# Two tables of step order changed: modulation products apart from their transposing products, selections and gates at other places

## The chip, the cores and the metric

The kernel runs on one core of a Trainium2 chip, as one program with one launch. The metric is the device time of that program in microseconds; lower is better. The engines are TensorE (PE, matrix products), VectorE (DVE), ScalarE (ACT), GpSimd (POOL) and SyncE (SP, which only issues transfers here). Each runs its own queue in order; they wait for one another on semaphores.

## The reference, cut to what matters

Two blocks on 256 latent tokens (and 256 context tokens) of width 1024, all in fp32.

The first block has two layers. In each, `silu(c) @ w_ada + b_ada` gives shift, scale and gate (the modulation); tokens are modulated and projected with `w_in`; then come three mixers: attention (8 heads on 2 key heads, RMS norm, rotary angles, softmax), a gated linear attention (GLA) forward and backward with log decays, and a gated spatial unit (SGU). Their outputs are multiplied by branch matrices and by sigmoid gates, summed, multiplied by `w_out`, and normed with the residual:

```
h = x * (1.0 + scale) + shift
y_attn, y_gla, y_sgu = attention(h), gla_forward(h) + gla_backward(h), sgu(h)
m = sigmoid(ga) * (ya @ w_br_attn) + sigmoid(gg) * (yg @ w_br_gla) + sigmoid(gs) * (ys @ w_br_sgu)
x = layer_norm(ALPHA * x + gate * (m @ w_out))
```

Layer 0 does this for latent and context tokens (512 in all); layer 1 only yields the latent ones, though keys, values and decays are still needed for all 512. The second block is a mixer (forgetting attention and a linear recurrence) and a mixture of 32 experts.

## The kernel before, in words

Four parts run one after the other: trunk layer 0, trunk layer 1, the mixer, the experts. Only the two trunk layers are touched.

A trunk layer is a list of named steps, built by `trunk_schedule(l)`: a fixed head, then the words of the table `ORDER_0` or `ORDER_1`, then the merging and closing steps. Each engine walks through the same list and issues what its own part of each step asks for; so the table sets the order on every engine at once. A step that an engine has no part in costs it nothing. The engines are not in step with each other: a step's parts are joined by semaphores alone.

Weights come from a stream of halves of 1 MB, fetched by SP into a ring of four. Its order is made from the tables too (`stream_order`: first use). Each dense weight is split into two parts: ACT copies the high part (L221), DVE subtracts it to get the residue (L229; four of them go to POOL). `with_splits` places these `split` steps two uses ahead of the product, and never before an `ada` step that stands ahead of that product. A dense product is then three products (L247, L248, L249).

PSUM has three pools of banks, taken in turn in the order in which TensorE opens them: four `proj` banks (PJ), two `score` banks (PS), two `turn` banks (PT). TensorE waits at an opening until the bank's last user has been copied out. So a step's place in the table also says which earlier job it has to wait for.

The steps that the change and the prediction speak of:

- `ada.l.n` (L702): a product with the modulation weights, in a PT bank; ACT copies its row out (L929). `adat.l.n` (L712): small products that turn this row into columns, in the next PT bank, after ACT's copy; DVE adds the bias (L1109). Layer 0 also does those of layer 1.
- `ag, ak, gq, gate, aq, gk, av, gv, sv, sg, su, gg`: dense products with parts of `w_in`; ACT copies most of them out, DVE `su`.
- `z`, `soft`, `decay`: the log decays; `soft` is a logarithm on ACT over 2048 elements (L1026), `decay` a subtraction and eight scans on DVE (L1173, L1179).
- `stat`, `rstd`, `rot`: head norms (a product, then logarithm L1000/L1004 and exponential L1009 on ACT, a product on DVE L1187) and the rotary products (L753, L1192 to L1195).
- `score.i` (L763): two products of queries and keys, in PS banks; DVE takes the minimum of the negated scores (L1200), ACT the exponential (L1034). `sums.i`: a reciprocal. `turn.i` (L771): transposes in PT banks, copied by ACT (L1043). `pv.i` (L783, L787): the product with the values. Layer 0 has 16 of these units (the last eight are twice as wide), layer 1 has 8.
- `key`, `keymul`, `keyt`, `kv`: the keys and the states of the GLA.
- `diag.p`, and for 14 numbers i (seven levels of two halves) `diff.i` (DVE L1261 and L1262, POOL L1366 and L1367, then two exponentials on ACT, L1060), `scale.i` (DVE L1265, POOL L1373), `pairs.i` (PE L826, DVE blends it in, L1276). `diff.i` has to wait for `pairs.(i-2)`, since it overwrites its operands.
- `svstat`, `svn`, `mix`: the norm and the product of the SGU. `query`, `out`, `ostat`, `orstd`, `silu`, `ysplit`, `merge_gate`: the end of the GLA and the beginning of the merging.

ACT holds one table of functions at a time; a change of function may put a load (ACT_TABLE_LOAD) in front of an instruction.

Of the kernel before, what the change touches and what calls it, by code (L numbers as in the profile page):

```python
# [410 lines left out]


ORDER_0 = """
ag.0 ag.1 ag.2 ag.3 ak.0 gq.0 gq.1 gate.0 aq.0 z.0 aq.1 z.1 stat.0 aq.2 z.2 aq.3 z.3 gk.0 stat.1 stat.2 gk.1
stat.3 stat.4 soft.0 av.0 rstd.0 rstd.1 rstd.2 rstd.3 rstd.4 gv.0 rot.0 rot.2 rot.3 decay.0 rot.1 gv.1 rot.4
decay.1 vt.0 gv.2 score.0 key.0 keymul.0 gv.3 sums.0 score.1 turn.0 sv.0 keyt.0 key.1 sv.1 keymul.1 ada.0.4
adat.0.4 sums.1 turn.1 sv.2 keyt.1 kv.0 kv.1 sv.3 svstat.0 kv.2 score.2 svn.0 pv.0 score.3 sg.0 sums.2 diag.0
turn.2 pv.1 sg.1 score.4 diag.1 sums.3 turn.3 sg.2 sg.3 pv.2 diff.0 score.5 sums.4 turn.4 scale.0 diff.1 pv.3
score.6 sgsilu.0 sums.5 diff.2 scale.1 pairs.0 turn.5 pv.4 su.0 score.7 scale.2 pairs.1 diff.3 sums.6 turn.6
ada.0.5 adat.0.5 pairs.2 pv.5 scale.3 diff.4 score.8 sums.7 mix.0 turn.7 scale.4 pairs.3 diff.5 score.9 su.1  # L420
sums.8 scale.5 pv.6 pairs.4 diff.6 ada.1.0 turn.8 adat.1.0 pv.7 score.10 scale.6 pairs.5 diff.7 sums.9 turn.9
pv.8 mix.1 su.2 scale.7 pairs.6 diff.8 score.11 sums.10 turn.10 scale.8 pairs.7 diff.9 pv.9 ada.1.1 adat.1.1
score.12 sums.11 pairs.8 scale.9 diff.10 turn.11 mix.2 pv.10 score.13 scale.10 pairs.9 diff.11 sums.12 su.3
turn.12 pv.11 scale.11 turn.13 pairs.10 diff.12 score.14 ada.1.2 adat.1.2 sums.13 scale.12 pairs.11 pv.12
mix.3 score.15 sums.14 diff.13 scale.13 ada.1.3 adat.1.3 pairs.12 turn.14 pv.13 sums.15 pairs.13 turn.15
ada.1.4 adat.1.4 pv.14 pv.15 query.0 ada.1.5 adat.1.5 ysplit.s.0 ysplit.s.1 ysplit.s.2 ysplit.s.3 gg.0 gg.1
out.0 silu.0 silu.1 out.1 ostat.0 ostat.1 gg.2 ostat.2 ostat.3 gg.3 orstd.0 orstd.1 orstd.2 orstd.3 silu.2
silu.3 merge_gate.s.0
"""


ORDER_1 = """
ak.0 gq.0 gq.1 gate.0 aq.0 z.0 aq.1 z.1 aq.2 z.2 aq.3 stat.1 stat.2 z.3 stat.0 gk.0 gk.1 stat.3 stat.4 soft.0
av.0 rstd.0 rstd.1 rstd.2 rstd.3 rstd.4 rot.1 rot.4 rot.0 rot.2 rot.3 vt.0 decay.0 decay.1 score.0 key.0
score.1 keymul.0 gv.0 gv.1 gv.2 gv.3 sums.0 keyt.0 key.1 turn.0 score.2 keymul.1 sv.0 sv.1 sv.2 sv.3 svstat.0
svn.0 keyt.1 kv.0 sums.1 sums.2 turn.1 kv.1 kv.2 diag.0 diag.1 pv.0 diff.0 scale.0 score.3 diff.1 mix.0
scale.1 turn.2 pairs.0 diff.2 pv.1 scale.2 pairs.1 score.4 diff.3 mix.1 diff.4 sums.3 scale.3 pairs.2 turn.3
scale.4 pv.2 pairs.3 diff.5 score.5 mix.2 sums.4 scale.5 pairs.4 turn.4 diff.6 scale.6 pv.3 pairs.5 diff.7
score.6 mix.3 scale.7 sums.5 pairs.6 diff.8 turn.5 scale.8 pairs.7 pv.4 diff.9 scale.9 score.7 pairs.8 sums.6
diff.10 scale.10 turn.6 pairs.9 diff.11 pv.5 scale.11 pairs.10 sums.7 diff.12 scale.12 turn.7 pairs.11 diff.13  # L440
pv.6 scale.13 pairs.12 pv.7 pairs.13 query.0 ysplit.s.0 ysplit.s.1 gg.0 gg.1 silu.0 silu.1 ysplit.s.2
ysplit.s.3 out.0 out.1 ostat.0 ostat.1 gg.2 ostat.2 ostat.3 gg.3 orstd.0 orstd.2 orstd.1 orstd.3 silu.3
merge_gate.s.0 silu.2
"""


# [1947 lines left out]
```

How the kernel before makes its waits and increments, by code:

```python
    def open(self, pe, name):  # L123
        n, size = len(self.job), len(self.tiles)
        assert name not in self.job, name
        self.job[name] = n
        if n >= size:
            pe.wait_ge(self.evac_sem[n % size], n // size)
        return self.tiles[n % size]
# [46 lines left out]
    def issue(self, sp, upto):  # L176
        upto = min(upto, len(STREAM))
        for n in range(self.issued, upto):
            if n >= NHALF:
                sp.wait_ge(*self.last_reader[n - NHALF])
            sp.dma_start(self.ring[:, n % NHALF, :], self.dram[n]).then_inc(self.landed[n % NHALF], 16)
        self.issued = max(self.issued, upto)
# [31 lines left out]
    def hi(self, act, slot, c):  # L215
        n = self.index[slot, c]
        kind = self.info[n][2]
        act.wait_ge(*self.W.has_landed(slot, c // 2))
        if n >= NPIECE:
            act.wait_ge(*self.used[n - NPIECE])
        act.activation(self.part(self.hi_ring[:, n % NPIECE, :], kind), self.raw(slot, c, kind), ACT.Copy)\
            .then_inc(self.hi_written, 1)
# [1 line left out]
    def lo(self, eng, name, slot, c):  # L224
        n = self.index[slot, c]
        _, _, kind, engine, _ = self.info[n]
        if engine == name:
            eng.wait_ge(self.hi_written, n + 1)
            eng.tensor_tensor(self.part(self.lo_ring[:, n % NPIECE, :], kind), self.raw(slot, c, kind),
                              self.part(self.hi_ring[:, n % NPIECE, :], kind).bitcast(F32), ALU.subtract)\
                .then_inc(self.lo_written[engine], 1)
```

## Time and profile before

| | us |
|---|---|
| median of 3 runs | 1442.76 |
| the three runs | 1442.76, 1439.63, 1442.8 |
| profiled execution | 1438.7 |
| its span, first to last instruction | 1436.9 |
| mean granted TensorE clock in it | 0.965 |
| PE / DVE / ACT / POOL busy | 1336.2 / 630.7 / 517.8 / 68.3 |
| layer 0, layer 1 (start to end, about) | 0 to 641, 641 to 1014 |
| mixer and experts (about) | 1014 to 1437 |

The times in the views are microseconds from the start of the span. A row of a timeline gives start, duration, engine, line, what is written and read, how many instructions are merged, and in brackets the idle time before it and what ended that. The granted clock is 1.00 at 2.4 GHz and 0.50 at 1.2 GHz, the only two levels in this trace; a mean between them mixes both.

### The profile page before, as it was taken

The numbers are of one execution on the slowest core, as the hardware profiler recorded it, in microseconds if no ns is written. First come the engines' busy times: TensorE is split into PE (matmuls) and PEld (weight loads), VectorE is DVE, ScalarE is ACT, GpSimd is POOL, SyncE is SP. The second block draws the span as 40 slices with busy tenths as digits, with TensorE's granted clock in tenths as the row PEclk, the third lists the DMA queues.
The fourth block names the chain that finished last, engine by engine and source line by source line (L and its number), as shares of the span: only waits on it lengthen the run. The fifth ranks groups of instructions, "written<-read, shape, count | busy, mean of one in ns | idle before, by whom it ended". The sixth has DMA issues, their size and how long they took to land. (4 is left out here: it accounts for less than half of the span.)

```text
span 1436.9 us, 19322 instructions
## 1 busy us (share of the span) xinstructions
PE 1336.2 (93%) x7954; PEld 1013.0 (70%) x7954; DVE 630.7 (44%) x1093; ACT 517.8 (36%) x877; POOL 68.3 (5%) x92
## 2 busy tenths in 40 slices
...
PEclk6999999898999999999998999999999999999998
...
GB/s 387 205 59 88 117 88 1 147 90 223 99 88 88 88 177 110 95 95 141 129 114 30 89 1 123 197 208 176 87 98 97 323 185 372 411 405 400 422 366 31
DMA packets 34222, 238.97 MB, mean 166 GB/s; under 512 B 4304, under 2 KB 4432, under 8 KB 6224
## 3 DMA queue, kind: packets, MB, share of 16 engines
...
q14 instruction: 28, 0.23, 0.0%
HBM read 236.59 MB, written 1.05 MB: 165 GB/s over the span
## 5 line engine op out<-in xcount | busy, mean ns | idle before, releaser
L229 DVE TENSOR_TENSOR pieces_lo<-weight_ring,pieces_hi 128x1024 fp32r<-128x1024 f32 x154 | 188.0, 1224 | 322.0 <-ACT pieces_hi L221 321.9
L247 PE MATMUL proj<-h_hi,pieces_hi 128*128 128x512 f32 (+1 forms) x816 | 289.4, 355 | 7.6 <-DVE h_lo L1145 3.6
L248 PE MATMUL proj<-h_lo,pieces_hi 128*128 128x512 f32 (+1 forms) x816 | 282.9, 347 | 0.0
L249 PE MATMUL proj<-h_hi,pieces_lo 128*128 128x512 f32 (+1 forms) x816 | 281.6, 345 | 0.0
L221 ACT ACTIVATE pieces_hi<-weight_ring 128x1024 fp32r<-128x1024 f32 x158 | 165.9, 1053 | 112.5 <-PE score L249 50.6
L247 PEld LDWEIGHTS proj<-h_hi,pieces_hi 128*128 128x128 f32 x816 | 154.7, 190 | 37.7 <-issue 10.5
L248 PEld LDWEIGHTS proj<-h_lo,pieces_hi 128*128 128x128 f32 x816 | 155.0, 190 | 21.2 <-issue 1.7
L249 PEld LDWEIGHTS proj<-h_hi,pieces_lo 128*128 128x128 f32 x816 | 155.2, 190 | 20.7
L1943 PE MATMUL turn<-expert_parts,e_gathered 128*64 128x256 f32 x768 | 85.3, 379 | 0.8 <-DVE e_gathered L2132 0.8
L1943 PEld LDWEIGHTS turn<-expert_parts,e_gathered 128*64 128x64 f32 x768 | 56.0, 137 | 32.4 <-issue 7.3
L1078 ACT ACTIVATE l_merge_gate<-proj 128x512 f32<-128x512 f32 (+1 forms) x48 | 23.6, 491 | 130.4 <-PE proj L249 130.4
L247 PE MATMUL proj<-pieces_hi,h_hi 128*128 128x512 f32 x160 | 65.7, 411 | 1.1 <-ACT l_probs_t L985 0.9
L248 PE MATMUL score<-l_y_lo,pieces_hi 128*128 128x512 f32 (+1 forms) x192 | 64.7, 337 | 0.0
L247 PE MATMUL score<-l_y_hi,pieces_hi 128*128 128x512 f32 (+1 forms) x192 | 64.4, 335 | 0.0
L249 PE MATMUL proj<-pieces_hi,h_lo 128*128 128x512 f32 x160 | 64.3, 402 | 0.0
L248 PE MATMUL proj<-pieces_lo,h_hi 128*128 128x512 f32 x160 | 64.2, 401 | 0.0
L249 PE MATMUL score<-l_y_hi,pieces_lo 128*128 128x512 f32 (+1 forms) x192 | 64.1, 334 | 0.0
L1503 PE MATMUL proj<-x_hT,weight_ring 128*128 128x256 f32 x256 | 58.2, 387 | 0.0
L1503 PEld LDWEIGHTS proj<-x_hT,weight_ring 128*128 128x128 f32 x256 | 49.4, 195 | 7.7 <-issue 0.8
L2143 DVE SCALAR_TENSOR_TENSOR e_out_lo<-score,e_slot_combine,e_out_hi 128x512 fp32r<-128x512 f32 x32 | 24.0, 751 | 52.8 <-ACT e_out_hi L2022 52.8
L2136 DVE TENSOR_TENSOR e_hidden<-e_silu,turn 128x256 f32<-128x256 f32 x16 | 6.7, 422 | 91.2 <-ACT e_silu L2010 91.2
L1034 ACT ACTIVATE l_probs<-score,l_small 128x512 f32<-128x512 f32 (+1 forms) x48 | 29.0, 609 | 43.9 <-DVE l_small L1200 43.8
(439 smaller groups left out, 2042.8 us busy)
## 6 DMA issues: line engine op xcount, KB each, us to landing
weight_ring<-in_stream SPq DMA_DIRECT2D x110, 1024.0 KB, 4.8
...
weight_ring<-in_experts SPq DMA_DIRECT2D x26, 1024.0 KB, 11.2
...
l_q<-in_ada_first SPq DMA_DIRECT2D x1, 1024.0 KB, 10.1
```

Source lines behind the costliest of these rows:

```text
L221: act.activation(self.part(self.hi_ring[:, n % NPIECE, :], kind), self.raw(slot, c, kind), ACT.Copy)\
L229: eng.tensor_tensor(self.part(self.lo_ring[:, n % NPIECE, :], kind), self.raw(slot, c, kind), self.part(self.hi_ring[:, n % NPIECE, :], ki ...
L247: pe.matmul(out, sh, mh, start=start, stop=False)
L248: pe.matmul(out, sh, ml, start=False, stop=False)
L249: return pe.matmul(out, sl, mh, start=False, stop=stop)
L1034: act.activation(PR[:, i % 2, u, 0:n], PS.tile(J("score", i, u))[:, 0:n], ACT.Exp, bias=small[:, i % 2, u:u + 1], scale=-1.0, accum_out=sm ...
L1078: act.activation(SGM[:, n % 4, 0:NT], PJ.tile(J("merge_gate", i))[:, 0:NT], ACT.Sigmoid)\
L1503: last = pe.matmul(acc[:, 0:T], w[:, k, i * P:(i + 1) * P], hT[:, k, :], start=(k == 0), stop=(k == KT - 1))
L1943: last = pe.matmul(acc[64 * f:64 * f + 64, u * 256:(u + 1) * 256], XG[:, q % 2, k, slots], w[:, n, f * 256:(f + 1) * 256], start=(k == 0), ...
L2136: dve.tensor_tensor(HG[:, i % 2], HS[:, i % 2], up, ALU.mult).then_inc(*PT.evac(J("gu", i)))
L2143: dve.scalar_tensor_tensor(OUT_L[:, i % 2, c], PS.tile(J("out", i, h))[:, :], CS[:, i // 4 % 2, i % 4:i % 4 + 1], OUT_H[:, i % 2, c].bitca ...
```

## The change

Only the two tables change. Both hold the same words as before. In layer 0 the moves are, in the main:

- `ak.0` and `gq.0` go ahead of `ag.2` and `ag.3` (this swaps two halves of the weight stream); `gk.1`, `aq.3`, `av.0` and the `z` and `stat` steps between them are arranged anew; `soft.0` goes between `rstd.3` and `rstd.4`.
- `turn.1` goes between `ada.0.4` and `adat.0.4`; `pairs.12` and `turn.14` between `ada.1.3` and `adat.1.3`; `pv.15` between `ada.1.5` and `adat.1.5`.
- `pairs.1` and `diff.3` go ahead of `su.0` and `score.7`; `score.8` ahead of `pv.5`; `turn.9` ahead of `score.10`; `score.11` behind `pv.9`; `mix.3` ahead of `pairs.11`; many `sums`, `scale` and `diff` steps by a few places.
- `query.0` goes behind `gg.0`, three of four `ysplit.s` behind `silu.0`, `orstd.0` behind `orstd.2`.

In layer 1: `decay.1` behind `score.0`; `keyt.0` ahead of `gv.3`; `keymul.1` behind `sv.0`; `diag.1` behind `pv.0`; `mix.1` and `diff.4` behind `pairs.2`; `diff.6` ahead of `turn.4` and `scale.5`; `diff.10` ahead of `sums.6`; `silu.3` behind `merge_gate.s.0`.

The lines of the diff that hold these moves (the rest of both tables is left out):

```diff
 ORDER_0 = """
-ag.0 ag.1 ag.2 ag.3 ak.0 gq.0 gq.1 gate.0 aq.0 z.0 aq.1 z.1 stat.0 aq.2 z.2 aq.3 z.3 gk.0 stat.1 stat.2 gk.1
-stat.3 stat.4 soft.0 av.0 rstd.0 rstd.1 rstd.2 rstd.3 rstd.4 gv.0 rot.0 rot.2 rot.3 decay.0 rot.1 gv.1 rot.4
-decay.1 vt.0 gv.2 score.0 key.0 keymul.0 gv.3 sums.0 score.1 turn.0 sv.0 keyt.0 key.1 sv.1 keymul.1 ada.0.4
-adat.0.4 sums.1 turn.1 sv.2 keyt.1 kv.0 kv.1 sv.3 svstat.0 kv.2 score.2 svn.0 pv.0 score.3 sg.0 sums.2 diag.0
-turn.2 pv.1 sg.1 score.4 diag.1 sums.3 turn.3 sg.2 sg.3 pv.2 diff.0 score.5 sums.4 turn.4 scale.0 diff.1 pv.3
-score.6 sgsilu.0 sums.5 diff.2 scale.1 pairs.0 turn.5 pv.4 su.0 score.7 scale.2 pairs.1 diff.3 sums.6 turn.6
-ada.0.5 adat.0.5 pairs.2 pv.5 scale.3 diff.4 score.8 sums.7 mix.0 turn.7 scale.4 pairs.3 diff.5 score.9 su.1
...
+ag.0 ag.1 ak.0 gq.0 ag.2 ag.3 gq.1 gate.0 aq.0 z.0 aq.1 stat.0 z.1 aq.2 z.2 z.3 gk.0 stat.1 aq.3 stat.3 av.0
+stat.4 stat.2 rstd.0 rstd.1 rstd.2 rstd.3 gk.1 soft.0 rstd.4 gv.0 rot.2 rot.3 decay.0 rot.1 rot.4 gv.1 rot.0
+decay.1 vt.0 gv.2 score.0 key.0 keymul.0 gv.3 sums.0 score.1 turn.0 sv.0 keyt.0 key.1 sums.1 sv.1 keymul.1
+ada.0.4 turn.1 adat.0.4 sv.2 keyt.1 kv.0 kv.1 sv.3 svstat.0 kv.2 score.2 svn.0 pv.0 score.3 sg.0 sums.2 sg.1
+pv.1 diag.0 turn.2 diag.1 sums.3 turn.3 sg.2 score.4 sg.3 pv.2 diff.0 score.5 sums.4 turn.4 scale.0 diff.1
+pv.3 score.6 sums.5 sgsilu.0 pairs.0 diff.2 scale.1 turn.5 pv.4 scale.2 pairs.1 diff.3 su.0 score.7 sums.6
+turn.6 ada.0.5 adat.0.5 pairs.2 scale.3 score.8 sums.7 pv.5 mix.0 turn.7 pairs.3 sums.8 diff.4 diff.5 scale.4
+score.9 su.1 scale.5 pairs.4 pv.6 diff.6 ada.1.0 turn.8 adat.1.0 pv.7 turn.9 scale.6 score.10 pairs.5 diff.7
+pv.8 mix.1 sums.9 su.2 scale.7 pairs.6 diff.8 turn.10 scale.8 sums.10 pairs.7 diff.9 pv.9 score.11 sums.11
+scale.9 ada.1.1 adat.1.1 score.12 pairs.8 diff.10 turn.11 sums.12 mix.2 pv.10 score.13 scale.10 pairs.9
...
+pv.12 sums.13 score.15 sums.14 diff.13 ada.1.3 pairs.12 scale.13 turn.14 adat.1.3 pv.13 pairs.13 turn.15
+ada.1.4 sums.15 adat.1.4 pv.14 ada.1.5 pv.15 adat.1.5 gg.0 query.0 ysplit.s.0 gg.1 out.0 silu.0 ysplit.s.1
+ysplit.s.2 ysplit.s.3 silu.1 out.1 ostat.0 ostat.1 gg.2 ostat.2 ostat.3 gg.3 orstd.1 orstd.2 orstd.0 orstd.3
+silu.2 silu.3 merge_gate.s.0
 """
 ORDER_1 = """
...
-av.0 rstd.0 rstd.1 rstd.2 rstd.3 rstd.4 rot.1 rot.4 rot.0 rot.2 rot.3 vt.0 decay.0 decay.1 score.0 key.0
-score.1 keymul.0 gv.0 gv.1 gv.2 gv.3 sums.0 keyt.0 key.1 turn.0 score.2 keymul.1 sv.0 sv.1 sv.2 sv.3 svstat.0
-svn.0 keyt.1 kv.0 sums.1 sums.2 turn.1 kv.1 kv.2 diag.0 diag.1 pv.0 diff.0 scale.0 score.3 diff.1 mix.0
-scale.1 turn.2 pairs.0 diff.2 pv.1 scale.2 pairs.1 score.4 diff.3 mix.1 diff.4 sums.3 scale.3 pairs.2 turn.3
-scale.4 pv.2 pairs.3 diff.5 score.5 mix.2 sums.4 scale.5 pairs.4 turn.4 diff.6 scale.6 pv.3 pairs.5 diff.7
...
+av.0 rstd.0 rstd.1 rstd.2 rstd.3 rstd.4 rot.1 rot.4 rot.0 rot.2 rot.3 vt.0 decay.0 score.0 decay.1 key.0
+score.1 keymul.0 gv.0 gv.1 gv.2 keyt.0 gv.3 sums.0 key.1 turn.0 score.2 sv.0 keymul.1 sv.1 sv.2 sv.3 svstat.0
+svn.0 keyt.1 kv.0 sums.1 sums.2 turn.1 kv.1 kv.2 diag.0 pv.0 diag.1 diff.0 scale.0 score.3 diff.1 mix.0 turn.2
+scale.1 pairs.0 diff.2 pv.1 scale.2 pairs.1 score.4 diff.3 sums.3 scale.3 pairs.2 mix.1 diff.4 turn.3 scale.4
+pv.2 pairs.3 diff.5 score.5 mix.2 pairs.4 diff.6 turn.4 sums.4 scale.5 scale.6 pv.3 pairs.5 diff.7 score.6
...
+out.0 out.1 ostat.0 ostat.1 gg.2 ostat.2 ostat.3 gg.3 orstd.0 orstd.2 orstd.1 orstd.3 merge_gate.s.0 silu.3
+silu.2
 """
```

## Rows read from the trace of the kernel before

**Rows 1.** The page: busy time by engine, and PE's clock in 40 slices.
```profile
PE 1336.2 (93%) x7954; PEld 1013.0 (70%) x7954; DVE 630.7 (44%) x1093; ACT 517.8 (36%) x877; POOL 68.3 (5%) x92
...
PEclk6999999898999999999998999999999999999998
```

**Rows 2.** Stretches: length, then busy PE, PEld, DVE, ACT, POOL; PEclk, DMA share, GB/s.
```profile
34.60:129.60 95.00, 95.00 (x379) 71.29 (x379) 26.56 (x31) 42.68 (x54) 0.00 (x0) 0.98 0.34 128
...
200.20:231.10 30.90, 30.90 (x186) 24.06 (x184) 13.41 (x28) 9.05 (x21) 0.00 (x0) 0.98 0.10 35
...
243.90:259.80 15.90, 11.86 (x61) 6.74 (x61) 7.21 (x16) 4.17 (x9) 3.44 (x5) 0.57 0.31 120
...
389.80:641.00 251.20, 251.10 (x1096) 203.42 (x1096) 108.19 (x125) 71.29 (x89) 0.00 (x0) 1.00 0.29 103
757.00:772.00 15.00, 6.78 (x14) 3.11 (x15) 13.45 (x28) 4.95 (x12) 0.00 (x0) 0.54 0.00 0
...
820.00:860.00 40.00, 32.24 (x343) 24.19 (x341) 36.42 (x110) 25.13 (x65) 20.20 (x40) 1.00 0.01 2
```

**Rows 3.** Waits of PE over the span: total us, times, longest.
```profile
PE turn L712 <- ACT l_y_gla L929: 11.6, 11, 2.4
PE score L763 <- ACT l_probs L1034: 8.3, 2, 7.3
```

**Rows 4.** Timeline of layer 1, 761 to 770 us, PE and DVE.
```profile
767.19 2.74 PE L763 MATMUL score<-l_k,l_q 64*128 64x512 f32 x4 [7.29 <-ACT l_probs L1034]
...
761.71 1.22 DVE L1173 TENSOR_TENSOR l_b_bwd<-l_b_bwd,l_decayed 128x1024 f32<-128x1024 f32 x1
762.97 2.63 DVE L1179 TENSOR_TENSOR_SCAN l_b_bwd<-consts,l_b_bwd 128x128 f32<-128x128 f32 x8
765.64 1.29 DVE L1200 TENSOR_REDUCE l_small<-score 128x1 f32<-128x512 f32 x2
```

**Rows 5.** Timeline of layer 1, PE: turn.0 and pv.0.
```profile
794.60 0.63 PE L771 MATMUL turn<-consts,l_probs 128*128 128x128 f32 x4 [0.50 <-ACT l_gla_att L1055]
...
818.48 1.09 PE L783 MATMUL proj<-l_probs_t,l_v 128*64 128x128 f32 x16 [0.92 <-issue]
```

**Rows 6.** Timeline of layer 0, PE: second half of turn.1.
```profile
177.13 0.41 PE L771 MATMUL turn<-consts,l_probs 128*128 128x128 f32 x2 [2.18 <-DVE modulation L1109]
```

**Rows 7.** Timeline of layer 0, ACT's load before rstd.0, PE's rot.1.
```profile
130.32 1.28 ACT L1009 ACT_TABLE_LOAD   x1
...
138.57 0.67 PE L753 MATMUL turn<-l_q,consts 128*128 128x256 f32 x2 [0.46 <-DVE l_probs L1192]
```

**Rows 8.** Timeline of layer 0, 233 to 255 us, PE, POOL and DVE.
```profile
233.44 1.16 PE L826 MATMUL proj<-l_decayed 64*128 64x128 f32 x16
...
235.61 0.39 PE L787 MATMUL proj<-consts,l_inverse_sums 128*64 128x128 f32 x4
...
236.03 1.47 POOL L1373 TENSOR_TENSOR l_decayed<-l_decayed,l_gla_k 128x512 f32<-128x512 f32 x1
...
236.27 1.78 DVE L1265 TENSOR_TENSOR l_decayed<-l_decayed,l_gla_q 128x512 f32<-128x512 f32 x1
...
247.23 3.64 PE L702 MATMUL turn<-weight_ring,silu_c 128*32 128x512 f32 x16 [3.32 <-ACT l_probs_t L1043]
...
253.38 2.08 PE L826 MATMUL proj<-l_decayed 64*128 64x128 f32 x16
```

**Rows 9.** Timeline of layer 0, PE: ada.1.1 and adat.1.1.
```profile
296.45 1.92 PE L702 MATMUL turn<-weight_ring,silu_c 128*32 128x512 f32 x16 [0.97 <-ACT l_probs_t L1043]
299.71 1.05 PE L712 MATMUL turn<-consts,l_y_gla 128*128 128x2 f32 x8 [1.33 <-ACT l_y_gla L929]
```

**Rows 10.** Timeline of layer 0, PE: adat.1.3 and pairs.12.
```profile
337.31 1.05 PE L712 MATMUL turn<-consts,l_y_gla 128*128 128x2 f32 x8 [2.21 <-ACT l_y_gla L929]
338.30 2.08 PE L826 MATMUL proj<-l_decayed 64*128 64x128 f32 x16
```

**Rows 11.** Timeline of layer 0, PE: start of gg.0.
```profile
356.54 0.47 PE L247 MATMUL proj<-h_hi,pieces_hi 128*128 128x512 f32 x1 [1.24 <-DVE pieces_lo L229]
```

More of the change, by code:

```diff
@@ L419 @@
-score.6 sgsilu.0 sums.5 diff.2 scale.1 pairs.0 turn.5 pv.4 su.0 score.7 scale.2 pairs.1 diff.3 sums.6 turn.6
-ada.0.5 adat.0.5 pairs.2 pv.5 scale.3 diff.4 score.8 sums.7 mix.0 turn.7 scale.4 pairs.3 diff.5 score.9 su.1
-sums.8 scale.5 pv.6 pairs.4 diff.6 ada.1.0 turn.8 adat.1.0 pv.7 score.10 scale.6 pairs.5 diff.7 sums.9 turn.9
-pv.8 mix.1 su.2 scale.7 pairs.6 diff.8 score.11 sums.10 turn.10 scale.8 pairs.7 diff.9 pv.9 ada.1.1 adat.1.1
-score.12 sums.11 pairs.8 scale.9 diff.10 turn.11 mix.2 pv.10 score.13 scale.10 pairs.9 diff.11 sums.12 su.3
```

14 lines of the change are left out of this document (4 added, 10 removed).

## The prediction, made before the change was run

> **What bounds the kernel now.** I read the page first. TensorE is busy for 93% of the span and its clock stands at full speed nearly throughout; DVE and ACT are busy for 44% and 36% [rows 1]. So only two things can be won: TensorE's waits, and the stretches at half clock. Next came the table by stretches [rows 2]. From 34.6 to 129.6 us, from 200.2 to 231.1 and in the whole closing part of layer 0 (389.8 to 641) TensorE is busy without a gap: 95.00 of 95.00, 30.90 of 30.90, 251.10 of 251.20. Reordering there can't pay. Between 243.9 and 259.8 it is busy for 11.86 of 15.90 us, at a mean clock of 0.57; between 757 and 772 for 6.78 of 15 us, at 0.54; between 820 and 860 for 32.24 of 40 us, while DVE is busy for 36.42 of 40: there DVE sets the pace. The list of waits puts 11.6 us on transposing products that wait for the copied modulation row, and 8.3 on score products that wait for ACT's exponential [rows 3]. The timelines then give the single places. No transfer ends one of these waits; the two swapped halves of the weight stream are both fetched at the start, so I put the swap at nothing.
>
> **Layer 1, the selection apart from the decay.** Score.1 sits 7.29 us waiting for a bank. ACT can free it only after DVE's minimum of score.0, and that one starts at 765.64, behind both decays. decay.1 begins at 761.71 and is 1.22 + 2.63 us. The table now puts score.0 ahead of it: 765.64 - 761.71 = 3.9 us earlier [rows 4]. What is then behind decay.1 on DVE (key.0, the minimum of score.1, keymul.0) is wanted by TensorE only behind gv.0 and gv.1, dense steps of 24 instructions at 0.23 us each by the closing part (251.10 for 1096) [rows 2], some 5.6 us. Against the 3.9: gv.0 starts at 765.9 instead of 769.9, in a clock that was half until 771.7 in this trace, so it may run at half for up to 4 us longer (a loss of 2.0) or get its clock back sooner (no loss). I take 0.6, so 3.3 net; bounds 1.9 and 3.9.
>
> Smaller places of layer 1. keyt.0 ahead of gv.3 lets its copies lie under gv.3: the 0.50 in front of turn.0 goes. pv.0 ahead of diag.1 removes 0.92 on TensorE, but DVE, which sets the pace from there, gains only its 0.4 [rows 5]. In the level loop diff.6 before scale.5, and diff.10 before sums.6, fill short DVE waits; DVE is idle for only 3.6 us of these 40 [rows 2], so 0.6, between 0 and 1. silu.3 behind merge_gate.s.0 saves a table switch where nobody waits: 0. Layer 1 together: 3.3 + 0.5 + 0.4 + 0.6 = **4.8**.
>
> **Layer 0, six places.**
> (a) ada.0.4, turn.1, adat.0.4. Now: 0.72 for the row copy (the smallest and commonest of the eleven waits of [rows 3]), then 2.18 because turn.1's second bank waits until DVE, behind two weight residues, has added the bias [rows 6]. Apart: turn.1.0 lies under the copy, but adat.0.4 now waits for ACT's copy of turn.1.0, which stands behind two weight splits. By the rows adat ends near 176.8 where turn.1 ended at 177.5: 0.7 gained, not 2.9. Bounds 0 and 2.3; the upper one adds that the clock, half after this wait, stays up.
> (b) soft.0 is put between rstd.3 and rstd.4. It is a logarithm among exponentials, and ACT loads a table of 1.28 us when it goes from one to the other. Two more loads delay rstd.4, and the residue of gv.2 and rot.2 behind it on DVE, by about 1.0 us (soft.0 and gk.1's copy no longer lie ahead of it in free time). TensorE has just gv.0 to hide this; the rot products wait 0.46 already. I take a loss of 1.0, between 0 and 2.6 (both loads) [rows 7].
> The Trainium skill, "ScalarE: Activation LUTs", section "Table sets: the hidden batching unit", says that one set holds both exp and ln, so that going from one to the other needs no further load. By that (b) would be free and the sum 1.0 better. The row shows the load between them here, so the measurement decides.
> (c) pairs.1 moves ahead of su.0. TensorE is free at 236.0, but pairs.1 needs POOL's product (ends 237.50) and DVE's (1.78 us beside POOL's, begun at 236.27). With pairs.0's blend put first on DVE it is ready between 237.65 and 238.45. I take 238.4: a new wait of 2.4 us. In return diff.3 and its exponential lie under su.0, ACT reaches turn.6 sooner, and the wait of 3.32 before ada.0.5 shrinks to 1.2. These two cancel (ada.0.5 at 247.8 instead of 247.2, a loss of 0.5). The gain, if any, is clock: after the 3.32 it was half until 259.7, where pairs took 2.08 instead of 1.16 and ada 3.64 instead of about 1.92; over the seven steps that is 5.5 us [rows 8, 2]. But the new wait of 2.4 may cost su.0 1.6, and 1.2 + 0.72 of waits with a thin transposing product between are still there. I take +3.0; bounds -2.1 and +5.5.
> The Trainium skill, "SBUF — State Buffer", section "Who interferes with whom", says that a DVE instruction with two SBUF inputs is shut out while GpSimd reads SBUF. By that DVE's difference and product would both come after 237.50, pairs.1 would be ready at 238.6 and the sum 0.2 worse; the 1.78 of the row fits it, but no row has this new order.
> (d) score.11 goes behind pv.9. ada.1.1 loses its 0.97 of wait, but ACT now copies its row behind diff.9 and score.11, and score.11 stands later. adat.1.1 follows near 10.1 us after su.2, against 9.5 now: -0.5, between -2 (a longer fall of the clock) and 0 [rows 9].
> (e) ada.1.3 and its transposing product: pairs.12 and the first half of turn.14 fit into the 2.21 of wait; both are ready. Some 0.5 of wait is left, so 1.7 is gained; and pairs.12 took 2.08, not 1.16, in the half clock that followed, turn.14 1.73 instead of 1.09: with the clock up 3.1. I take 3.0, bounds 1.7 and 3.1 [rows 10].
> (f) pv.15 between ada.1.5 and its product fills the 0.72, and ada.1.5 stands 1.3 earlier, so the residue of gg.0, on which 1.24 us are spent, comes earlier too: 1.2, bounds 0.7 and 1.4 [rows 11]. query.0 and three ysplits, now later on ACT, have gg.0 and gg.1 (11 us) for cover. If that cover went, out.0 would wait for two exponentials and two products, about 4 us.
> Everything else in layer 0 (ag and ak swapped, z and stat, gk.1, score.4, turn.9, the sums) lies where TensorE has no wait, or under a dense product: 0.
> Layer 0: 0.7 - 1.0 + 3.0 - 0.5 + 3.0 + 1.2 = **6.4**.
>
> **Sum.** 4.8 + 6.4 = 11.2 us. The profiled execution took 1438.7 (span 1436.9 and 1.8 around it) and would take 1427.5. It lies 4.1 below the median of the runs, 1442.76, which would become 1431.6. I name the middle, **1429.5**; on this scale the kernel before stands at 1440.7. The likeliest case's own range is 1424 to 1435. The mixer and the experts are unchanged and only start earlier.
>
> **Rivals.**
> 1. The clock stays up. A wait of 0.97 was passed at full speed in this trace, ada.1.1 taking 1.92 behind it [rows 9]; those of 2.2 and more were followed by half clock, as pairs.12 and pairs.2 show by 2.08 [rows 10, 8]. If (c) keeps it (+2.5), (a) too (+1.5), and (b) costs nothing (+1.0) with layer 1 at its upper bound (+0.6): 5.6 better, 1424. Against it: the new 2.4 in (c).
> 2. The waits only change places. Apart or not, adat waits for the same ACT queue; (a), (c) and (d) show that a step put between meets the next bank. If all of layer 0 comes to nothing and layer 1 gives only its lower bound of 1.9: 1438.8, no change.
> 3. Slower, by one mechanism: the clock. If it falls at the new wait before pairs.1 and stays half past 250, as it did after the 3.32, then (c)'s gain of 3.0 is lost, and 0.5 + 5.5 comes on top; the same persistence after (d)'s 2.6 us costs 4 more instead of 0.5 (3.5 net), and after score.0 the remaining 1.4. 11.2 - 3.0 - 6.0 - 3.5 - 1.4 = -2.7: about 1443.5. It decides at the first pairs behind su.0: 2.08 or 1.16. For it: the fall that lasted 16 us. Against it: the shorter falls of this trace ended within one or two steps, and a dense su.0 follows here.
>
> **Chances.** Forecast 0.45, rival 1 0.22, rival 2 0.20, rival 3 0.13. Differences below 0.3% (4.3 us) can't be told from no change. Forecast and rival 1 are faster, with a third of rival 2: 0.73; the rest of rival 2 and a part of rival 3: 0.18; slower 0.09. The range 1418 to 1442 takes in both ends of (c) and of layer 1.
>
> **What would show it.** In the profile after: the wait before score.1 of layer 1 at 3.4 us, not 7.3; a new wait near 2 before pairs.1 of layer 0, and ada.0.5's at 1.2; pairs.2 at 1.16; before adat.1.3 under 0.6; before adat.1.1 about 2.6; turn.1's second half released by ACT; a wait of about 1 between the rots. Wrong would be: pairs.2 again at 2.08, gv.0 of layer 1 beginning later than 8 us after score.0, or gv.1 of layer 0 more than 2 us late.

## The result, and the profile after

The changed kernel ran at 1425.62 us median of four runs (1425.14 to 1430.01), beside 1442.13 for the kernel before (four runs, 1439.63 to 1442.8): ratio 0.9911, 95% interval 0.989 to 0.9932, so 13 us faster by that ratio (the two medians alone lie 16.5 apart). The profiled execution took 1425.68 with a span of 1423.9, which is 13.0 less than the profiled one of before. A second set of six runs gave 1426.94 beside 1438.54 (0.9917, 0.9887 to 0.9947). The forecast was 1429.5.

The page of the kernel after: busy time by engine, and PE's clock in 40 slices (to set beside [rows 1]).

```profile
PE 1332.7 (94%) x7954; PEld 1013.1 (71%) x7954; DVE 629.9 (44%) x1093; ACT 519.1 (36%) x878; POOL 66.4 (5%) x92
...
PEclk7999999999999999998998999999999999999998
```

The same 7954 products; their busy time fell by 3.5 us, the rest of the 13.0 is waiting that went. The stretches of after: length, then busy PE, PEld, DVE, ACT, POOL; PEclk, DMA share, GB/s.

```profile
743.00:760.60 17.60, 13.12 (x28) 6.71 (x29) 17.10 (x41) 2.39 (x6) 0.00 (x0) 0.52 0.00 0
...
820.00:850.00 30.00, 23.91 (x257) 19.07 (x256) 27.25 (x81) 18.65 (x48) 14.12 (x28) 1.00 0.01 2
389.80:632.90 243.10, 243.10 (x1065) 197.21 (x1064) 104.59 (x122) 66.81 (x84) 0.00 (x0) 1.00 0.29 104
228.10:259.10 31.00, 25.55 (x205) 17.83 (x204) 20.90 (x44) 17.76 (x38) 11.24 (x14) 0.94 0.14 52
```

The closing part of layer 0 is still full. The stretch from the last gate to score.9 in layer 0 (228.1 to 259.1) now has a clock of 0.94. The same steps of before took 34.46 us, from 228.3 to 262.8; the stretch at a clock of 0.57 [rows 2] lies within them. The neighbourhood of layer 1's first scores is still at half clock (0.52).

The waits of PE, summed over the span (total, times, longest):

```profile
PE turn L712 <- ACT l_y_gla L929: 9.8, 8, 3.2
...
PE score L763 <- ACT l_probs L1034: 4.3, 2, 3.3
```

The waits of the transposing products fell by 1.8 us from 11.6, those of the scores by 4.0 from 8.3 [rows 3]: score.1's wait went from 7.29 to 3.26. Its timeline, PE and DVE:

```profile
755.37 2.74 PE L763 MATMUL score<-l_k,l_q 64*128 64x512 f32 x4 [3.26 <-ACT l_probs L1034]
...
753.81 1.29 DVE L1200 TENSOR_REDUCE l_small<-score 128x1 f32<-128x512 f32 x2
755.01 1.22 DVE L1173 TENSOR_TENSOR l_b_bwd<-l_b_bwd,l_decayed 128x1024 f32<-128x1024 f32 x1
```

DVE's minimum of score.0 now stands ahead of the second decay [rows 4]. In layer 0, around the new place of pairs.1:

```profile
235.26 0.39 PE L787 MATMUL proj<-consts,l_inverse_sums 128*64 128x128 f32 x4
238.03 1.84 PE L826 MATMUL proj<-l_decayed 64*128 64x128 f32 x16 [2.38 <-DVE l_decayed L1265]
239.80 0.79 PE L247 MATMUL proj<-h_hi,pieces_hi 128*128 128x512 f32 x1
...
249.02 1.92 PE L702 MATMUL turn<-weight_ring,silu_c 128*32 128x512 f32 x16 [1.25 <-ACT l_probs_t L1043]
251.66 1.05 PE L712 MATMUL turn<-consts,l_y_gla 128*128 128x2 f32 x8 [0.72 <-ACT l_y_gla L929]
252.64 1.16 PE L826 MATMUL proj<-l_decayed 64*128 64x128 f32 x16
```

There is a new wait of 2.38 us in front of pairs.1; ada.0.5 waits 1.25 instead of 3.32, and pairs.2 takes 1.16, not 2.08 [rows 8]. The other places, in order of time: adat.0.4; score.11, ada.1.1 and adat.1.1; pairs.12 to adat.1.3; gg.0:

```profile
177.43 1.02 PE L712 MATMUL turn<-consts,l_y_gla 128*128 128x2 f32 x8 [1.75 <-ACT l_probs_t L1043]
...
290.48 1.13 PE L763 MATMUL score<-l_k,l_q 64*128 64x512 f32 x4
291.54 1.92 PE L702 MATMUL turn<-weight_ring,silu_c 128*32 128x512 f32 x16
296.63 1.87 PE L712 MATMUL turn<-consts,l_y_gla 128*128 128x2 f32 x8 [3.17 <-ACT l_y_gla L929]
298.43 2.08 PE L763 MATMUL score<-l_k,l_q 64*128 64x512 f32 x4
...
333.30 1.16 PE L826 MATMUL proj<-l_decayed 64*128 64x128 f32 x16
334.40 0.66 PE L771 MATMUL turn<-consts,l_probs 128*128 128x128 f32 x4
335.40 0.63 PE L771 MATMUL turn<-consts,l_probs 128*128 128x128 f32 x4 [0.34 <-ACT l_y_gla L929]
335.89 1.02 PE L712 MATMUL turn<-consts,l_y_gla 128*128 128x2 f32 x8
...
350.33 0.47 PE L247 MATMUL proj<-h_hi,pieces_hi 128*128 128x512 f32 x1 [0.79 <-DVE pieces_lo L229]
```

adat.0.4 now waits 1.75 for ACT's copy of turn.1 [rows 6]; adat.1.1 waits 3.17 instead of 1.33, and what follows runs at half clock [rows 9]; adat.1.3's 2.21 is down to 0.34 in front of turn.14 [rows 10]; gg.0's 1.24 is 0.79 [rows 11].

**The gain by places.** Where each step's last product ends, in both profiled executions, gives the ledger (us gained by the profile after):

| stretch, TensorE | gained | term of the forecast |
|---|---|---|
| start to gv.0 of layer 0 | -0.7 | 0 |
| (b) gv.0 to gv.1 | -0.8 | -1.0 |
| (a) ada.0.4 to sv.2 | +2.1 | +0.7 |
| (c) last sg to score.9 | +3.5 | +3.0 |
| (d) ada.1.0 to su.3 | -2.2 | -0.5 |
| (e) ada.1.3 to turn.15 | +3.4 | +3.0 |
| (f) turn.15 to gg.0 | +1.1 | +1.2 |
| layer 1, last aq to av.0 | +1.6 | 0 |
| layer 1, decay.1 behind score.0 | +3.6 | +3.3 |
| layer 1, gv.1 to gg.0 | +0.9 | +1.5 |

With 0.6 behind gg.0 of layer 1, and stretches between these lines that cancel to within 0.1, these are the 13.0 us but for rounding. Two lines aren't the order's doing: the start (the first half clock ended at 40.4 us instead of 37.9, further into the first dense products, though it was 20.5 us long and not 23.9) and layer 1's +1.6 (a short fall of the clock, 3.4 us near 727 us, in front of av.0; of these two profiles only that of before has it, and in the repeated profile of the changed kernel it is back). The experiments below show how much of (a) and (c) is of the same kind.

### The profile page after: what moved, and what is told of

Same layout as the page of the kernel before. It is cut to its first block and busy times, and to the rows that moved or that the text cites. A ratio compares the mean times of both kernels' runs of the same rounds, so it can differ in the third digit from the quotient of the medians.

```text
span 1423.9 us, 19322 instructions
## 1 busy us (share of the span) xinstructions
PE 1332.7 (94%) x7954; PEld 1013.1 (71%) x7954; DVE 629.9 (44%) x1093; ACT 519.1 (36%) x878; POOL 66.4 (5%) x92
## 6 DMA issues: line engine op xcount, KB each, us to landing
l_q<-in_ada_first SPq DMA_DIRECT2D x1, 1024.0 KB, 10.2
```

## The experiments

All kernels of a group ran on one chip, each beside runs of the kernel before: 1440.26 median of 16 for the first four below (layer1_table, layer0_table, decay_only, before_fill), 1441.26 of 9 for the next four, 1438.54 of 15 for the last four. The table below is worked out from the profiled execution of each: the length in us of a stretch of TensorE, from the end of one step's last product to the end of another's, and after the slash how much of it stood at half clock. "after, again" is the changed kernel run once more. The experiments refer to these rows and columns.

```
                          A             B             C             D             E            F            G
                          ada.0.4-sv.2  sg.3-score.9  ada.1.0-su.3  score.14-     ada.1.3-     L1: aq.3-    L1: gk.1-
                                                                    ada.1.3       gg.0         gk.1         gv.1
before                    11.79 / 3.4   34.46 / 13.7  42.90 /  6.8  14.74 / 6.8   27.27 / 3.4  17.48 / 3.4  41.63 / 17.1
layer1_table              11.79 / 3.4   34.46 / 13.7  42.90 /  6.8  14.75 / 6.8   27.28 / 3.4  17.49 / 3.4  37.85 / 13.7
decay_only                11.79 / 3.4   34.42 / 13.7  42.89 /  6.8  14.74 / 6.8   27.26 / 3.4  17.49 / 3.4  37.87 / 13.7
before_fill (c)           12.67 / 6.8   30.51 /  0.0  42.85 /  6.8  13.20 / 3.4   30.29 /10.2  17.51 / 3.4  41.49 / 17.1
layer0_table              11.27 / 3.4   30.97 /  3.4  45.08 / 10.2  13.11 / 3.4   22.89 / 0.0  17.47 / 3.4  41.68 / 20.5
after                      9.72 / 0.0   31.00 /  3.4  45.05 / 10.2  14.67 / 6.8   22.79 / 0.0  15.91 / 0.0  38.01 / 17.1
after, again              12.70 / 6.8   30.97 /  3.4  45.23 / 10.2  13.08 / 3.4   22.90 / 0.0  17.46 / 3.4  38.19 / 10.2
score.11 back (d)         12.63 / 6.8   30.97 /  3.4  42.62 /  6.8  14.71 / 6.8   24.34 / 3.4  17.48 / 3.4  37.95 / 13.7
fill at adat.1.1 (d)      12.67 / 6.8   30.97 /  3.4  41.99 /  3.4  13.11 / 3.4   22.90 / 0.0  17.46 / 3.4  38.09 / 13.7
adat.1.3 together (e)      9.71 / 0.0   30.98 /  3.4  45.04 / 10.2  14.67 / 6.8   25.91 / 3.4  17.53 / 3.4  37.63 / 13.7
pairs.1 back (c)           9.73 / 0.0   28.87 /  0.0  43.61 /  6.8  13.11 / 3.4   22.91 / 0.0  17.48 / 3.4  38.03 / 17.1
pairs.1 back, again       12.67 / 6.8   32.75 / 10.2  43.62 /  6.8  13.11 / 3.4   22.91 / 0.0  17.47 / 3.4  38.06 / 13.7
apart                     12.64 / 6.8   30.87 /  6.8  45.53 / 10.2   9.44 / 0.0   22.22 / 0.0  15.92 / 0.0  28.23 /  0.0
apart, pairs.1 early       9.71 / 0.0   30.97 /  3.4  46.04 / 10.2   9.44 / 0.0   22.17 / 0.0  17.48 / 3.4  29.69 /  6.8
```

Code that is the same in all of these kernels varies as well, and each total with it: the mixer and the experts, from their first product to the end, take 415.7 to 419.2 us in these 14 profiles, and the first dense product stands between 33.1 and 34.9 us. So a single place is sized by its column; the medians can only tell larger sums.

**One layer's table at a time.** Each kernel takes one table from the change and one from before.

```diff
 layer1_table:                 layer0_table:
-ORDER_0 of after             -ORDER_1 of after
+ORDER_0 of before            +ORDER_1 of before
```

> Layer 0 as before, layer 1's new table alone. Theory A (each place gives its own part, and the parts add up): in the two profiles layer 1 from its first projection to its end is 6.2 us shorter in the kernel after, 1.6 of it a fall of the clock near 727 us that only the trace of before has and that isn't the change's. So 4.6 to 6.2 us less than before, 1436 to 1437.5. Theory B (the gains of the two layers need one another, since clock and transfers carry over): less than 3 us, or more than 8. Score.1's wait should be 3.3 instead of 7.3 us, turn.0's 0.50 gone.

> Layer 0's new table alone, layer 1 as before. Theory A: layer 0 gives 6.2 us in the profiles (7.5 without its start, which was 1.3 us late there by the clock alone), so 1434.5 to 1436 against 1442. Theory B: less than 3 us. The sum of this run's gain and that of the kernel with layer 1's table alone should be the whole change's gain (13 by the profiles, 16.5 by the medians) to within 2.5 us.

Layer 1's table alone: 1431.66 (1430.81 to 1432.36), ratio 0.9938, 0.9921 to 0.9954, or 8.9 us. Layer 0's alone: 1430.57 (1429.46 to 1431.74), ratio 0.993, 0.9913 to 0.9946, or 10.1. Both tables gain. Their sum is 19 and the whole change 13 by its ratio; with 2.4 us of interval on either side of each part and 3 on the whole, the two just touch. Both totals missed what was expected of them (1436 to 1437.5, and 1434.5 to 1436), and layer 1's fell in the band of theory B, more than 8. The columns speak for theory A: with layer 1's table alone columns A to E are as before, and with layer 0's alone column G is. From aq.3 of layer 1 to that layer's end layer 1's table gives 4.8 us. The profile as a whole is 6.5 shorter, 1.5 of it in the start, which this table doesn't touch; what the rest of the 8.9 is, these runs don't tell.

**decay.1 behind score.0 alone**, in the table of before.

```diff
-decay.0 decay.1 score.0 key.0
+decay.0 score.0 decay.1 key.0
```

> The kernel before with one word moved: decay.1 of layer 1 behind score.0. Theory A: 3.7 us less, most of layer 1's gain; score.1 waits 3.3 us instead of 7.3, gv.0 ends 3.7 earlier. Rival (DVE, which now runs decay.1 later, delays key.0 and the weight residue of gv.2, and the gain is given back before gv.3): less than 1.5 us, with a new wait before gv.2.

1435.99 (1432.69 to 1437.66, seven runs), ratio 0.9972, 0.9958 to 0.9986: 4.0 us, 2.0 to 6.0. Column G falls by 3.76, and from gv.1 to gg.0 of layer 1 nothing comes back (80.13 us beside 80.12). The profile as a whole is only 1.9 shorter than that of before; 1.0 more is in the mixer and the experts, which the swap doesn't touch. In its trace:

```profile
758.31 2.08 PE L763 MATMUL score<-l_k,l_q 64*128 64x512 f32 x4 [1.20 <-DVE l_q L1195]
763.64 2.74 PE L763 MATMUL score<-l_k,l_q 64*128 64x512 f32 x4 [3.26 <-ACT l_probs L1034]
```

The same 3.26 as in the changed kernel: one swap of two words is the largest sure piece of the change.

**(c) The clock fill in the kernel before.** 24 products of no use, 256 columns each, are issued in front of ada.0.5, in the wait of 3.32 us.

```diff
+if i == (0, 5):
+    busy = PJ.tile(J("pv", 4))
+    pe.wait_ge(*PJ.evacuated(J("pv", 4)))
+    keep_busy(pe, busy, HH[:, 0, 0:256], 256, 24)
```

> The kernel before with 24 idle products of 256 columns on TensorE (about 3.1 us, to a bank that is written anew later) in the wait of 3.3 us before ada.0.5. No step comes earlier; only TensorE is busy during the wait. Theory A (what (c) gave is clock): the clock stays at full speed behind it, pairs.2 takes 1.16 instead of 2.08, and su.1 ends 4 to 5.5 us earlier; the kernel takes 1437 to 1438. Rival (the 16 us behind the wait are slow by ACT and DVE, and the clock is no matter): su.1 ends where it did, the time is 1442.

```profile
245.39 3.11 PE L255 MATMUL proj<-h_hi 128*128 128x256 f32 x24
248.97 1.93 PE L706 MATMUL turn<-weight_ring,silu_c 128*32 128x512 f32 x16 [0.47 <-ACT l_probs_t L1047]
251.61 1.05 PE L716 MATMUL turn<-consts,l_y_gla 128*128 128x2 f32 x8 [0.72 <-ACT l_y_gla L933]
252.60 1.16 PE L830 MATMUL proj<-l_decayed 64*128 64x128 f32 x16
...
258.80 1.79 PE L767 MATMUL score<-l_k,l_q 64*128 64x512 f32 x4 [0.56 <-ACT l_probs L1038]
```

With nothing moved, ada.0.5 takes 1.93 instead of 3.64 and pairs.2 1.16 instead of 2.08 [rows 8], and column B falls from 34.46 to 30.51. So the clock behind this wait alone is worth 4.0 us in the old order, enough for the 3.5 that the ledger books for (c). It isn't worth the 5.5 of the prediction, since a wait of 0.56 before score.9 appears, which the half clock had covered. The new order has more in store once the clock stays up: with pairs.1 late (below) column B took 28.87 with no half clock, and score.9 didn't wait. That 1.6 comes from other moves between sg.3 and score.9 (score.8 ahead of pv.5 among them), which the prediction put at nothing; which of them isn't isolated.

But the whole kernel gained nothing that the runs can tell: 1438.62 (ten runs), ratio 0.9996, 0.9982 to 1.0009; theory A's 1437 to 1438 isn't shown. Its profile is 1.8 us longer than that of before. 3.0 come back in column E, where the clock stood at half for 10.2 us instead of 3.4; D gained 1.5 in the same way; 2.9 more are in the mixer and the experts, and 0.9 each in column A and in the start, all of it code that stands behind or ahead of the fill and is the same in both.

**(c) undone in the changed kernel**, twice: pairs.1 and diff.3 go back behind su.0 and score.7.

```diff
-pv.4 scale.2 pairs.1 diff.3 su.0 score.7 sums.6
+pv.4 su.0 score.7 scale.2 pairs.1 diff.3 sums.6
```

> The kernel after with (c) alone undone: pairs.1 and diff.3 behind su.0 and score.7 again. Theory A: the wait of 2.4 before pairs.1 goes, that before ada.0.5 is 3.3 again, the clock falls for more than 10 us behind it, su.1 ends 3 to 4 us later: 1428.5 to 1430. Rival (the order of pairs.1 changes nothing, only the clock's luck between two profiles): 1425.5, and in the profile either clock.

> The changed kernel with pairs.1 and diff.3 back behind su.0 and score.7, a second time. Theory A: 1421 to 1423, because the 2.4 us wait ahead of pairs.1 goes, while the wait of ada.0.5 grows from 1.3 to 3.3 and pairs.2 waits less, and no clock fall follows the wait. Rival B (luck): 1424 to 1427. Rival C: 1428.

> The changed kernel once more, beside the three others, so that the place of pairs.1 is sized within one set of runs. Theory A (step (c) costs): 1425 to 1427, 3 to 5 us above the version with pairs.1 back behind score.7. Rival B (the 1421.7 of that version was a lucky draw of the clock): both within 1.5 us of each other. Rival C (the prediction's step (c), the early pairs.1 gains 3): the changed kernel is the faster of the two.

First: 1421.72 (1420.01 to 1422.41, four runs), ratio 0.9869, 0.9837 to 0.9902. Second, the same kernel: 1429.71 (1421.06 to 1431.78, ten runs), ratio 0.9928, 0.9904 to 0.9951, with the changed kernel beside it at 1426.94. So the first result, 4 us faster than the changed kernel, was luck. The second set alone lies nearest to rival C (the changed kernel 2.8 us faster); all executions together, 1427.3 median of 14 with pairs.1 late and 1426.1 of 10 with it early, lie within the 1.5 us of rival B. The two profiles show what luck decides. First run, then second, same program:

```profile
244.41 1.93 PE L702 MATMUL turn<-weight_ring,silu_c 128*32 128x512 f32 x16 [3.32 <-ACT l_probs_t L1043]
247.05 1.05 PE L712 MATMUL turn<-consts,l_y_gla 128*128 128x2 f32 x8 [0.72 <-ACT l_y_gla L929]
248.03 1.16 PE L826 MATMUL proj<-l_decayed 64*128 64x128 f32 x16
```

```profile
250.01 3.64 PE L702 MATMUL turn<-weight_ring,silu_c 128*32 128x512 f32 x16 [3.33 <-ACT l_probs_t L1043]
254.37 1.87 PE L712 MATMUL turn<-consts,l_y_gla 128*128 128x2 f32 x8 [0.72 <-ACT l_y_gla L929]
256.17 2.08 PE L826 MATMUL proj<-l_decayed 64*128 64x128 f32 x16
```

The same wait of 3.3 us was passed at full clock in one and followed by half clock in the other (column B: 0 and 10.2 us of it, 28.87 and 32.75 in length). With pairs.1 early, column B is 30.97 to 31.00 in all seven profiles, each with the same 3.4 us. At full clock the late place is the shorter one. Both profiles with pairs.1 late also have 1.5 us less in column C, where the fall of 3.4 us behind adat.1.0 is missing; whether the place of pairs.1 does that, two profiles don't show.

**(d) undone, and its wait filled.** score.11 goes back ahead of turn.10; and, in another kernel, 22 products of no use are issued between ada.1.1 and adat.1.1.

```diff
-diff.8 turn.10 scale.8 sums.10 pairs.7 diff.9 pv.9 score.11 sums.11
+diff.8 score.11 sums.10 turn.10 scale.8 pairs.7 diff.9 pv.9 sums.11
```

```diff
+if i in ((1, 1),):
+    acc = PT.open(pe, modulated_t(*i))
+    keep_busy(pe, acc, HH[:, 0, 0:256], 256, 22)
...
-acc = PT.open(pe, modulated_t(*i))
+if i not in ((1, 1),):
+    acc = PT.open(pe, modulated_t(*i))
```

> The kernel after with (d) alone undone: score.11 stands ahead of turn.10 again. Theory A: the wait before adat.1.1 splits again (near 1.0 and 1.3 instead of 3.2), the clock falls once or not at all instead of for 6.8 us, and score.12 and pairs.8 come 2 to 3 us earlier: 1422.5 to 1424. Rival (the loss of 2.4 between su.2 and su.3 is where the clock happened to fall and not the order): the same time as after within 1 us.

> The kernel after with 22 idle products of 256 columns (some 2.8 us) in the wait of 3.2 us between ada.1.1 and adat.1.1; no step comes earlier by it. Theory A: the clock no longer falls for 6.8 us behind it; score.12 and pairs.8 run at full speed, su.3 ends 2.0 to 3.4 us earlier: 1422.5 to 1423.6. Rival (what is lost there is the wait itself, behind ACT's queue): the same time as after.

Undone: 1426.51 (1423.06 to 1429.41), ratio 0.9895, 0.9857 to 0.9934. Filled: 1425.08 (1423.87 to 1426.39), ratio 0.9894, 0.9861 to 0.9927. Locally both show the cost: column C goes from 45.05 to 42.62, and to 41.99. With the fill the wait is covered and the clock stays up:

```profile
294.18 2.89 PE L255 MATMUL turn<-h_hi 128*128 128x256 f32 x22
297.41 1.05 PE L716 MATMUL turn<-consts,l_y_gla 128*128 128x2 f32 x8 [0.34 <-ACT l_y_gla L933]
298.39 1.13 PE L767 MATMUL score<-l_k,l_q 64*128 64x512 f32 x4
```

So (d) costs 2.4 us where it stands: behind adat.1.1 the clock is at half for 3.4 us with score.11 back, and for 6.8 in every profile with the change's order there and no fill. The medians don't show the 2.4 (1426.51 and 1425.08, beside 1425.62 and 1426.94 for the changed kernel). Both theories A, 1422.5 to 1424 and 1422.5 to 1423.6, came true at the place and not in the total; by the total, each rival (the same time as the changed kernel) fits. In the profile with score.11 back, columns D and E have 1.6 and 1.4 more than in the repeated profile of the changed kernel.

**(e) undone**: adat.1.3 right behind ada.1.3 again.

```diff
-ada.1.3 pairs.12 scale.13 turn.14 adat.1.3
+ada.1.3 adat.1.3 pairs.12 scale.13 turn.14
```

> The kernel after with (e) alone undone: adat.1.3 right behind ada.1.3. Theory A: the wait of 2.2 us is back (0.34 in the kernel after), the clock falls behind it, pairs.12 takes 2.08 again: 3.0 us more, 1428.6. If only the wait counts: 1.9 more, 1427.5. Rival: pairs.12 and turn.14 are wanted by ACT and DVE at the same time as before, so less than 1 us more.

1429.6 (1424.87 to 1432.1, six runs), ratio 0.9918, 0.9894 to 0.9943; column E goes from 22.79 to 25.91, 3.1 us, with a wait of 1.93 back. The half clock came one step later than theory A had it: pairs.12 still takes 1.16, turn.14 and pv.13 stand at half clock. The total can't confirm the 3.1 (ratio 0.9918, beside 0.9911 and 0.9917 for the changed kernel):

```profile
335.36 1.05 PE L712 MATMUL turn<-consts,l_y_gla 128*128 128x2 f32 x8 [1.93 <-ACT l_y_gla L929]
336.35 1.16 PE L826 MATMUL proj<-l_decayed 64*128 64x128 f32 x16
337.44 1.97 PE L771 MATMUL turn<-consts,l_probs 128*128 128x128 f32 x8
339.34 1.79 PE L783 MATMUL proj<-l_probs_t,l_v 128*64 128x128 f32 x16
```

**The idea carried on.** pairs.1 late, and something ready put into each wait that was left.

```diff
-ada.0.5 adat.0.5 pairs.2            -diff.6 ada.1.0 turn.8 adat.1.0 pv.7 turn.9
+ada.0.5 pairs.2 adat.0.5            +diff.6 ada.1.0 pv.7 turn.8 adat.1.0 turn.9
-pv.9 score.11 sums.11 scale.9 ada.1.1 adat.1.1
+pv.9 ada.1.1 score.11 sums.11 scale.9 adat.1.1
-ada.1.2 adat.1.2 mix.3 pairs.11     -ada.1.4 sums.15 adat.1.4 pv.14
+ada.1.2 mix.3 pairs.11 adat.1.2     +ada.1.4 sums.15 pv.14 adat.1.4
-av.0 rstd.0 rstd.1 rstd.2 rstd.3 rstd.4 rot.1                       (layer 1)
+rstd.0 rstd.1 rstd.2 rstd.3 rstd.4 av.0 rot.1
-score.0 decay.1 key.0 score.1 keymul.0 gv.0 gv.1
+score.0 gv.0 decay.1 key.0 score.1 keymul.0 gv.1
```

> pairs.1 back behind score.7, and the change's own idea carried on at each place where the changed kernel still waits: score.11 between ada.1.1 and adat.1.1 (wait 3.17), mix.3 and pairs.11 between ada.1.2 and adat.1.2 (2.37), pairs.2 before adat.0.5 (0.72), pv.7 before turn.8 (1.23), pv.14 before adat.1.4 (0.72); in layer 1 gv.0 between score.0 and score.1 (3.26) and the five rstd ahead of av.0 (rot.1's 3.81). Theory A (each wait is on the path, a product of the same length laid in it gives the whole of it, up to the product's length): 3.3 + 1.3 + 1.3 to 2.5 + 2.1 + 0.7 + 0.9 + 0.7, some 10 to 11, so 1411 to 1413 from 1422. Rival B (waits only change places, as behind pairs.1): under 4, so 1418 or more. Rival D (fewer waits also keep the granted clock up between 296 and 331 and between 743 and 760): 1407 to 1409.

> The same as the version beside it, with pairs.1 and diff.3 ahead of su.0 and score.7, as in the change. Theory A (step (c) costs its own wait): 2 to 4 us slower than with pairs.1 behind score.7. Rival B (the place is worth nothing, the clock draws decide): within 1 us. Rival C (prediction): 3 faster.

1412.89 (1408.07 to 1418.53, six runs), ratio 0.9823, 0.9789 to 0.9857, 25 us under the kernel before and 14.0 under the changed kernel beside it; with pairs.1 early 1413.46 (1409.93 to 1415.54), ratio 0.9824, 0.9794 to 0.9855, so its place made no difference here either. The stretch of column G, first of the changed kernel again, then of this one:

```profile
733.90:772.00 38.10, 28.04 (x100) 19.22 (x99) 24.10 (x48) 14.32 (x26) 0.00 (x0) 0.87 0.14 48
```

```profile
729.80:758.00 28.20, 24.29 (x100) 16.64 (x99) 20.44 (x45) 10.92 (x19) 0.00 (x0) 1.00 0.11 38
```

The same 100 products, 9.9 us sooner: idle time went from 10.1 to 3.9, and 3.75 of busy time went with the half clock, since gv.0 lies under DVE's minimum and ACT's exponentials of `rstd` no longer wait for av.0's copy (rot.1 waited 3.81 for them, and doesn't wait now). Column D gave 3.6: mix.3 and pairs.11 cover ACT's copy, and 0.19 of a 2.37 wait is left. Column C gave nothing (45.5 beside 45.2). There the wait only changed places: adat.1.1's 3.17 became 1.17, with 0.50 before ada.1.1 and a new 2.56 before score.12, which waits for ACT to have read score.11:

```profile
293.04 1.93 PE L702 MATMUL turn<-weight_ring,silu_c 128*32 128x512 f32 x16 [0.50 <-ACT l_probs_t L1043]
294.89 1.13 PE L763 MATMUL score<-l_k,l_q 64*128 64x512 f32 x4
297.19 1.05 PE L712 MATMUL turn<-consts,l_y_gla 128*128 128x2 f32 x8 [1.17 <-ACT l_y_gla L929]
300.81 2.74 PE L763 MATMUL score<-l_k,l_q 64*128 64x512 f32 x4 [2.56 <-ACT l_probs L1034]
```

The expectation's 10 to 11 us started from 1422; beside the changed kernel the gain was 14.0, and 9.9 + 3.6 = 13.5 us lie in columns G and D. (E and F give 0.7 and 1.5 more, and the start, where the clock differs, takes 2.2 back.) In columns G and D that is theory A (each wait is on the path) with rival D (the clock comes with it), at a higher base; in column C it is rival B (the waits change places), which for the whole would have left it above 1418. This version beats both kernels.

## Why the prediction came out as it did

**Right:** the reading that only waits and half clock can be won, and in layer 1 the chain behind it. The wait of score.1 was forecast at 3.4 and was 3.26. The step (3.3) gave 3.6 in the ledger, with 17.1 us of half clock in column G on both sides, and 4.0 alone. Nothing was late in its place; gv.0 begins 8.01 us after score.0 (758.03 and 750.02), at the border of 8 that was named as a sign of being wrong.

**(e) right:** 3.0 forecast, 3.4 in the ledger, 3.1 when undone; 0.5 of wait forecast, 0.34 left. **(f)** 1.2 forecast, 1.1 in the ledger. **(b)** -1.0 forecast, -0.8 in the ledger: rot.1 waits 0.99, because ACT loads a table before soft.0 and another before rstd.4.

```profile
131.05 1.28 ACT L1026 ACT_TABLE_LOAD   x1
132.34 2.01 ACT L1026 ACTIVATE l_decayed<-l_decayed,consts 128x2048 f32<-128x2048 f32 x1
134.37 1.28 ACT L1009 ACT_TABLE_LOAD   x1
...
138.99 0.67 PE L753 MATMUL turn<-l_q,consts 128*128 128x256 f32 x2 [0.99 <-DVE l_probs L1192]
```

**(a) a size off, by the clock.** With the same 3.4 us of half clock, column A is 11.79 in the old order and 11.27 in the new one, 0.5 against the 0.7 forecast. With 6.8 us in both it is 12.67 in the old order (in the kernel with the fill, which stands behind this stretch) and 12.63 to 12.70 in the new one, so nothing. The +2.1 of the ledger holds some 1.5 of a clock that happened to stay up; in the repeated profile it fell for 6.8 us and the place took 0.9 more than in the profile of before. The bounds of 0 to 2.3 missed that side.

**(c) the waits right, the worth not shown.** The new wait (forecast 2.4, measured 2.38), the one left before ada.0.5 (1.2 and 1.25) and pairs.2 (1.16) came as forecast, and the ledger shows 3.5 for 3.0. The size of the new wait is in part luck, for its terms were others: POOL's product ended at 236.75, and DVE's own took 0.68 us behind it, not 1.78 beside it [rows 8], while the difference ahead of it took 1.36 (0.79 in the trace of before).

```profile
235.49 1.26 POOL L1373 TENSOR_TENSOR l_decayed<-l_decayed,l_gla_k 128x512 f32<-128x512 f32 x1
...
235.68 1.36 DVE L1261 TENSOR_TENSOR l_decayed<-l_b_fwd 128x256 f32<-128x256 f32 x1
...
237.29 0.68 DVE L1265 TENSOR_TENSOR l_decayed<-l_decayed,l_gla_q 128x512 f32<-128x512 f32 x1
```

And the step took the long half clock behind the old wait for a thing of pairs.1's place. In the old table of layer 0 it is steady: 13.7 us in three of three profiles without the fill, and 3.4 in seven of seven with the new table as it is. In the new tables the late place had 0 once and 10.2 once, and the median of the kernel was 3.9 better, then 2.8 worse, and 0.6 better in the third pair, where the late place had 6.8 of half clock. What pairs.1's early place may buy is an even result (5.4 us between the slowest and the fastest of 10 executions, against 11.8 in 14; in the third pair 5.6 against 10.5, six each), and no gain that these runs can tell; which other move of the new table took the rest of the long fall away isn't shown. Why the clock falls behind the 3.3 us wait in one execution and not in another stays open.

**(d) the mis-sized term:** -0.5 forecast, -2.2 in the ledger, -2.4 when undone. The wait was put at 2.6 and was 3.17, so adat.1.1 began 10.5 us behind su.2 (forecast 10.1, before 9.5); and the fall behind it lasts 6.8 us, where adat.1.1 takes 1.87, score.12 2.08 and pairs.8 1.91. That is rival 3's mechanism, at this one place.

**The level loop:** keyt.0 gave 0.7 for 0.5, while pv.0 before diag.1 and the diff steps gave 0.2 for 1.0. DVE was busy for 36.42 of the 40 us before [rows 2] and is for 27.25 of 30 now, the same nine tenths: swapping two of its short steps moved no idle time out.

**The sum:** 11.2 forecast, 13.0 between the two profiles. The difference is +1.4 in (a), -1.7 in (d), +0.5 in (c), +0.8 in (b), (e), (f) and the decay together, -0.6 in layer 1's end, -0.7 and +1.6 of luck, and 0.6 behind the layers. At what repeats (a 0.5 at most, b -0.8, column B 3.5, d -2.4, e 3.1, f 1.1, decay 3.7, layer 1's end 0.9) the order is worth 9.6 us or a little less, just under the low end of the first interval (9.8 to 15.9 us) and inside the second (7.6 to 16.3). So the forecast of 11.2 lies between what repeats and what the two profiles show; some 3.4 of their 13.0 are the clock's luck. Of the rivals, the first (the clock stays up, 1424) is what (a) and (c) show in the first profile; the second (waits change places) is what (a) and (d) do. The slower one didn't come about: at the new wait before pairs.1 the clock fell for 3.4 us and was back under su.0.
